# The opening of a mixed conv and attention network: first norm's sums on VectorE, X in two transfers, eight banks, norm vectors first

## The reference

```python
def rms_norm(x, g):
    y = x * lax.rsqrt(jnp.mean(x * x, axis=-1, keepdims=True) + NORM_EPS)
    return y * g

hn = rms_norm(x, a_norm[0])
proj = hn @ a_w_in[0]                     # 1024 x 6144
val, glu_gate, z = jnp.split(proj, 3, axis=-1)
u = val * jax.nn.sigmoid(glu_gate)        # then 31 taps along the tokens, per channel
```

## Time and profile before

| | |
|---|---|
| median of 3 runs | 2649.19 us (2649.11 to 2651.65) |
| the profiled execution, its own time | 2649.69 us |
| its span | 2648.0 us, 31953 instructions |
| busy, share of the span | PE 97%, PEld 79%, DVE 57%, ACT 47%, POOL 57% |
| DMA | 276.51 MB, mean 104 GB/s |

### The profile page before, as it was taken

The page is one execution under the profiler, slowest core; times in us unless marked ns, Lnnn a source line. Parts: engine busy times, 40 slices in busy tenths (PEclk is TensorE's granted clock), DMA queues, the critical chain, the costliest instruction groups (busy, mean ns, idle before and its releaser), DMA issues.

```text
span 2648.0 us, 31953 instructions
## 1 busy us (share of the span) xinstructions
PE 2578.6 (97%) x12164; PEld 2081.0 (79%) x12164; DVE 1521.2 (57%) x2431; ACT 1231.5 (47%) x1939; POOL 1513.8 (57%) x926
## 2 busy tenths in 40 slices
PE   8999999999999899999999999989999999999998
PEld 6877787877777687888888787878877778788887
DVE  4999883145675824444450799976498743523202
ACT  4888544245555534222232598654335553423222
POOL 2799765444444365444455299966635547645652
PEclk9999999999999999999999999999999999999999
DMA  5776424444344123333333577533422242233221
GB/s 145 179 179 145 112 96 87 92 95 70 78 78 69 62 80 87 104 96 96 97 96 103 119 180 170 143 96 96 120 96 71 78 136 100 80 99 101 103 96 48
DMA packets 295128, 276.51 MB, mean 104 GB/s; under 512 B 17653, under 2 KB 258511, under 8 KB 294976
## 3 DMA queue, kind: packets, MB, share of 16 engines
q1 hardware_dynamic: 280880, 223.94, 30.9%
q0 software_dynamic: 14096, 50.53, 9.2%
HBM read 228.75 MB, written 5.84 MB: 89 GB/s over the span
## 4 chain that ended last, share of the span: by engine, by line
PE 84%; DVE 9%; ACT 3%; issue 2%; POOL 1%; DMA 0%; DVEq 0%; POOLq 0%; ACTq 0%
PE ps L64 82%; DVE AR L81 4%; PE ps L67 2%; DVE AR L73 2%; DVE HL L81 1%; ACT L70 1%; ACT HT L70 1%; ACT AR L70 1%; DVE X L73 1%; POOL WL L73 0%; POOL AR L73 0%; DMA AR<-in_x 0%; POOL HL L73 0%; DVE AR L77 0%; ACT HH L70 0%
## 5 line engine op out<-in xcount | busy, mean ns | idle before, releaser
L73 POOL TENSOR_TENSOR WL<-WR,WH 128x1024 fp32r<-128x1024 f32 x329 | 831.9, 2549 | 815.0 <-ACT WH L70 815.0
L64 PE MATMUL ps<-HH,WH 128*128 128x512 f32 x3080 | 1228.8, 399 | 22.9 <-POOL HL L73 12.4
L64 PE MATMUL ps<-HL,WH 128*128 128x512 f32 x3080 | 1202.5, 390 | 0.0
L64 PE MATMUL ps<-HH,WL 128*128 128x512 f32 x3080 | 1100.1, 390 | 0.0
L64 PEld LDWEIGHTS ps<-HH,WH 128*128 128x128 f32 x3080 | 580.2, 188 | 167.3 <-issue 33.0
L64 PEld LDWEIGHTS ps<-HL,WH 128*128 128x128 f32 x3080 | 580.7, 189 | 123.6 <-issue 7.7
L64 PEld LDWEIGHTS ps<-HH,WL 128*128 128x128 f32 x3080 | 580.0, 188 | 122.3
L70 ACT ACTIVATE WH<-WR 128x1024 fp32r<-128x1024 f32 (+1 forms) x405 | 409.0, 1047 | 493.0 <-PE ps L64 439.2
L81 DVE SCALAR_TENSOR_TENSOR ps<-AR,CW,ps 128x512 f32<-128x512 f32 x654 | 454.5, 752 | 8.8 <-ACT ps L70 1.5
L73 POOL TENSOR_TENSOR AR<-AR 128x512 f32<-128x512 f32 x200 | 307.9, 1846 | 11.1 <-ACT AR L70 3.8
L70 ACT ACTIVATE AR<-ps 128x512 f32<-128x512 f32 (+3 forms) x265 | 132.2, 523 | 268.2 <-PE ps L64 169.0
(11 more groups left out here) (169 smaller groups left out, 2255.7 us busy)
## 6 DMA issues: line engine op xcount, KB each, us to landing
WR<-in_a_w_in SPq DMA_DIRECT2D x96, 512.0 KB, 5.2
WL<-WR POOLq DMA_DIRECT2D x76, 512.0 KB, 5.8
WR<-in_c_w_in SPq DMA_DIRECT2D x64, 512.0 KB, 5.3
WR<-in_a_w_out SPq DMA_DIRECT2D x16, 1024.0 KB, 4.8
WR<-in_b_w_in SPq DMA_DIRECT2D x16, 1024.0 KB, 8.5
WR<-in_b_w_in SPq DMA_DIRECT2D x32, 512.0 KB, 12.3
WR<-in_w_mlp_in SPq DMA_DIRECT2D x16, 1024.0 KB, 5.4
WR<-in_w_mlp_out SPq DMA_DIRECT2D x16, 1024.0 KB, 4.9
```

Source lines behind the costliest of these rows:

```text
L64: return Op(None if self.e is None else self.e.matmul(o, l, r, start=first, stop=last, skip_group_check=True))
L73: return Op(None if self.e is None else self.e.tensor_tensor(o, a, b, op))
```

## The change

X comes in two DMAs of 1 MB. The small vectors come right behind X (VA) and behind chunk 0 (VB), with semaphores of their own; chunk 1 comes after them, then the conv rows as before. TensorE turns X by blocks of tokens into all eight banks (`X_BANK`), with no sums between. VectorE squares and sums each block of tokens along its row in one instruction, straight from `XIN`. ScalarE copies tiles 0 to 5 out of the banks and VectorE tiles 6 and 7, after the norm vector. ScalarE loads its root table first and takes the root after three copies. Chunk 0 joins the summed chunks, so its WL comes from a DMA add; ScalarE splits its half 0 after the root and its half 1 inside the loop over HH, after HH 3; the conv taps are copied after HH 1. The turn of the conv taps now stands behind the spread.

```diff
         def summed(i, n):
-            return any(f < i < f + KE + (KE // 2 if n == 0 else 0) for f in FIRST_A)
+            return i == 0 or any(f < i < f + KE + (KE // 2 if n == 0 else 0) for f in FIRST_A)
...
+        X_BANK = [7, 4, 5, 6, 3, 2, 1, 0]
+        BY_SCALAR = 6
         def wait_x(eng, m, k):
             if m == 0:
-                eng.wait_ge(x0, k)
+                eng.wait_ge(*((sq_made, "x", k) if k < BY_SCALAR else (x0, k)))
...
         def mean_square_vector(dve, m):
-            dve.wait_ge(sq_summed, m, KD - 1)
-            rsqrt_vector(dve, ("ms", m), banks[0][:, 0:NB], NB, 1.0 / D)
+            if m:
+                dve.wait_ge(sq_summed, m, KD - 1)
+            else:
+                dve.wait_ge(x0, "sum", NB - 1)
+            rsqrt_vector(dve, ("ms", m), banks[0][:, 0:NB] if m else small(NB, "x_sum"), NB, 1.0 / D)
...
                 act.act(hs(HH, k), tiles[k % 4], ACT.Copy).then_inc(hh, gen, k)
+                if j == 0 and k == 1:
+                    vectors_scalar(act)
+                if j == 0 and k == 3:
+                    split_hi(act, 0, (1,))
...
         def setup_sync(sp):
-            sp.dma(t3(XIN, NB), x[0].rearrange("(b p) d -> p b d", p=P)).then_inc(x_in, by=16)
-            load_chunk(sp, 0)
-            load_chunk(sp, 1)
+            for n in range(2):
+                sp.dma(t3(XIN, NB)[:, 2 * n:2 * n + 2, :],
+                       x[0, 2 * n * P:2 * (n + 1) * P, :].rearrange("(b p) d -> p b d", p=P)).then_inc(x_landed[n], "x", by=16)
             o = 0
             for name, ap, n in VA_ROWS:
-                sp.dma(S_A[o:o + n, :], ap).then_inc(small_in, name, by=16)
+                sp.dma(S_A[o:o + n, :], ap).then_inc(v_landed, name, by=16)
                 o += n
+            load_chunk(sp, 0)
             for n, (name, ap) in enumerate(VB_ROWS):
                 sp.dma(S_B[32 * n:32 * n + 32, :], ap.rearrange("a (k p) -> (a k) p", p=P)).then_inc(
-                    small_in, name, by=16)
+                    v_landed, name, by=16)
+            load_chunk(sp, 1)
...
         def setup_tensor(pe):
             pe.wait_ge(consts, "ident")
-            pe.wait_ge(x_in)
-            for k in range(KD):
-                b = banks[1 + k % 3]
-                if k >= 3:
-                    pe.wait_ge(x0, k - 3)
-                for tb in range(NB):
-                    op = pe.turn(b[:, tb * P:(tb + 1) * P], XIN[:, tb * D + k * P:tb * D + (k + 1) * P], ident[:, :])
-                op.then_inc(xt_made, k)
-                if k:
-                    sum_square(pe, 0, k - 1)
-            sum_square(pe, 0, KD - 1)
-            pe.wait_ge(small_in, "all")
+            for tb in range(NB):
+                pe.wait_ge(x_landed[tb // 2], "x")
+                for k in range(KD):
+                    op = pe.turn(banks[X_BANK[k]][:, tb * P:(tb + 1) * P], XIN[:, tb * D + k * P:tb * D + (k + 1) * P],
+                                 ident[:, :])
+                    if tb == NB - 1:
+                        op.then_inc(xt_made, k)
+            pe.wait_ge(v_landed, VB_ROWS[-1][0])
+            wait_x(pe, 0, X_BANK.index(4))
             pe.turn(banks[4][:, 0:NVA], S_A[0:NVA, :], ident[0:NVA, 0:NVA])
             pe.turn(banks[4][:, 128:224], S_B[0:96, :], ident[0:96, 0:96]).then_inc(vec_turned, "v")
+            wait_x(pe, 0, X_BANK.index(7))
+
+        def vectors_tensor(pe):
+            pe.wait_ge(small_in, "all")
+            wait_x(pe, 0, X_BANK.index(6))
             for j in range(2):
...
         def setup_vector(dve):
             dve.memset(TABLE[32:33, :], NEG).then_inc(tab_neg)
-            for k in range(KD):
+            sums = small(NB, "x_sum")
+            for tb in range(NB):
+                dve.wait_ge(x_landed[tb // 2], "x")
+                row = XIN[:, tb * D:(tb + 1) * D]
+                dve.ttr(SQUARED[tb], row, row, 1.0, 0.0, ALU.mult, ALU.add, sums[:, tb:tb + 1]).then_inc(x0, "sum", tb)
+
+        def rest_of_x_vector(dve):
+            for k in range(BY_SCALAR, KD):
                 dve.wait_ge(xt_made, k)
-                dve.copy(xs(k), banks[1 + k % 3][:, :]).then_inc(x0, k)
+                dve.copy(xs(k), banks[X_BANK[k]][:, :]).then_inc(x0, k)
...
         def setup_scalar(act):
-            for k in range(KD):
-                square(act, 0, k)
-                if k == 3:
-                    split_hi(act, 0)
+            act.wait_ge(consts, "ones")
+            act.act(small(1, "table"), ones[:, 0:1], ACT.Sqrt)
+            for k in range(BY_SCALAR):
+                act.wait_ge(xt_made, k)
+                act.act(xs(k), banks[X_BANK[k]][:, :], ACT.Copy).then_inc(sq_made, "x", k)
+                if k == 2:
+                    rsqrt_scalar(act, ("ms", 0), NB)
+                    split_hi(act, 0, (0,))
...
             normalise_tensor(pe, j)
             if j == 0:
+                vectors_tensor(pe)
                 biases_tensor(pe)
...
             if j == 0:
                 vectors_vector(dve)
+                rest_of_x_vector(dve)
...
-            rsqrt_scalar(act, ("ms", j), NB)
-            if j == 0:
-                vectors_scalar(act)
+            if j:
+                rsqrt_scalar(act, ("ms", j), NB)
             normalise_scalar(act, j)
```

More of the change, by code:

```diff
@@ L691, in build_program @@
         GD = ar(10000, NDIST)
+        SQUARED = [ar(12000 + tb * D, D) for tb in range(NB)]
         SM0 = HT[:, 0:P]
         scratch = nc.dram_tensor("bias_by_distance", (16, NDIST), F32).ap()
+        x_landed = [x_in, sig("s_gin")]
+        v_landed = sig("stored")
         def setup_sync(sp):
-            sp.dma(t3(XIN, NB), x[0].rearrange("(b p) d -> p b d", p=P)).then_inc(x_in, by=16)
-            load_chunk(sp, 0)
-            load_chunk(sp, 1)
+            for n in range(2):
+                sp.dma(t3(XIN, NB)[:, 2 * n:2 * n + 2, :],
+                       x[0, 2 * n * P:2 * (n + 1) * P, :].rearrange("(b p) d -> p b d", p=P)).then_inc(x_landed[n], "x", by=16)
             o = 0
             for name, ap, n in VA_ROWS:
-                sp.dma(S_A[o:o + n, :], ap).then_inc(small_in, name, by=16)
+                sp.dma(S_A[o:o + n, :], ap).then_inc(v_landed, name, by=16)
                 o += n
+            load_chunk(sp, 0)
             for n, (name, ap) in enumerate(VB_ROWS):
                 sp.dma(S_B[32 * n:32 * n + 32, :], ap.rearrange("a (k p) -> (a k) p", p=P)).then_inc(
-                    small_in, name, by=16)
+                    v_landed, name, by=16)
+            load_chunk(sp, 1)
             for j in range(2):
```

## The result

In 20 runs of each on one chip the changed kernel takes 2646.26 us in the median (2645.23 to 2649.90), the kernel before 2651.24 (2649.11 to 2654.64). The ratio is 0.9982, 95% interval 0.9975 to 0.9989: 4.8 us faster, from 2.9 to 6.6. The forecast was 3.8 us faster, 2645.4.

What follows compares the result with a forecast made beforehand. TensorE bounds the kernel, so only the start of its unbroken work counts: its last-tile products end at 40.6 instead of 44.44, 3.8 us less. From the median 2649.19 that gives 2645.4, own range 2643.1 to 2647.4 (chance 0.45).

Steps and rivals of the forecast that it cites:

- The opening's arithmetic: Opening: X's turns from 6.15 to 13.9, sums by 11.7 at worst, root at 14.1, spread ending at 18.2.
- The landing, t = 25.9: Last small rows, awaited by TensorE's turn of the conv taps, land at 25.9 instead of 23.1, 2.8 us for the add.
- the toll: Chunk 0's DMA add overlaps the conv rows' transfers and delays them, between nothing and 2.8 us; taken as 2.8.
- the drip: Conv row transfers (`a_conv_w`) on SP's queue at some 78 GB/s, table and one-hot rows within, taken as 6.65 us.
- The chain after the landing: From 25.9: turns and two copies to 28.55, HH 2 and 3 to 29.85, GpSimd's low parts, HL 7 at 39.2.
- The rival with no toll: The add takes no turns from the conv rows' transfers; time 2645.4 - 2.8 = 2642.6, chance 0.18.
- the one in which the rows don't bind: Conv rows in by 20, only GpSimd's wait for half 1 counts; gain 11.6, 2637.6, chance 0.12.
- The hold: GpSimd's add of chunk 0's half 1 stands ahead of its low parts, HL 7 at 39.2 not 36.6; costs 2.6.
- TensorE's pace: Of TensorE's 21 products from 34.4, 7 at 0.425 us and 14 at 0.229, so the end is at 40.6.
- What is late next: Chunk 2's issue moves from 23.84 to 37.7, landed by 48.5 at worst; 4 us of cover are left.
- The rival of a gain given back: Chunk 2's lateness eats VectorE's and ScalarE's slack; TensorE waits 3.8 us or so in the conv stage; 2649.2, chance 0.17.
- the slower one: SP's ten issues behind the chunks held 2.26 us each, landing at 35.5; 5.8 slower, 2655.0, chance 0.08.

Runs made afterwards that it cites:

- the kernel without the sum: Changed kernel with chunk 0 subtracted by GpSimd again, no DMA add; ratio to before 0.9978 (0.9969 to 0.9987).
- the four that only move the landing: Changed kernel with conv rows ahead of chunk 1 (ratio to before 0.9984), in 112 + 12 (0.9974), rows and tables ahead (0.9965), or four row transfers (0.9958).
- with 112 + 12 rows: Changed kernel with each conv row transfer of 124 rows cut into 112 and 12, 16 transfers; ratio to before 0.9974 (0.9963 to 0.9985).
- with TensorE kept busy: Changed kernel with 16 more matmuls on TensorE, results thrown away, in its idle time before the conv taps' turn; ratio to before 0.9980 (0.9971 to 0.9990).

## Why the prediction was right

**What bounds, and that the gain stays.** Right. TensorE sets the conv stage, and the 3.3 us at 41.26 are 3.3 at 308 and at 2275.

**The opening's arithmetic.** Right in order, and off by 1 us in time, off the path: X landed as forecast (turns from 5.98), but TensorE needed 6.59 us for 32 turns and not 7.75, so the root came at 13.0 and the spread at 15.0, not at 16.1.

**The landing, t = 25.9.** Measured 25.8, from parts that were not all right, so its closeness is in part luck. Without the add the rows landed at 23.5 and not at 23.1, 0.4 later; the toll is 2.3 (shown by the kernel without the sum), not 2.8, 0.5 less. The two errors went against each other. The length of the drip was taken over from the kernel before without a cause; its 124 rows set it. The toll was priced as turns that the drip loses while the add runs. The drip lost none from 17 to 19 us and stood still from 20 to 21, so the size was about right and the way to it was not: turns taken a packet at a time, the rule that the prediction cites, do not show in this trace. The issues of SP are held longer than I thought, the last at 20.45. The chain after the landing took 13.07 us to the end of HL 7 in the changed kernel (13.3 forecast) and 13.07 or 13.08 in the four that only move the landing. Its first step was mis-added: eight turns at 0.223 and a copy of 0.58 make 2.4 us, where the prediction has 2.65, and measured are 2.5. The rival with no toll falls, and so does the one in which the rows don't bind: they were forecast as 2642.6 and 2637.6.

**The hold.** Forecast 2.6, measured 2.8 to 3.1 (first product, HL 7).

**TensorE's pace.** The term that was mis-sized: I took 7 of 21 products at 1.2 GHz, and it was 12. That is 5 x 0.2 = 1.0 us. The 21 began at 33.81 and not at 34.4, which gave back 0.6; 0.3 came on top, since the first of them took 0.60 and not 0.425 and the pace did not rise at once. So the first product ended at 41.26 instead of 40.6.

**What is late next.** Chunk 2 went out at 36.19, and no new wait of TensorE came of it in the conv stage. The rival of a gain given back fell with the positions above, the slower one with SP's issues: ten took 9.6 us (11.18 to 20.81), not 22.6.

The forecast was 3.8 us, the trace shows 3.3 in the opening and 4.2 in the span, the runs 4.8 with 2.9 to 6.6. The 0.9 between opening and span lies behind 2611, with the clock; where the rest of the 4.8 comes from is not shown, since each kernel has one trace. That 2645.4 lies so near the measured 2646.26 is in part luck as well: the prediction started from 2649.19, the median of three runs, 2.1 us below the 2651.24 of twenty, and its gain was 1.0 to 1.2 too small.

## What to carry to other kernels

When an opening is reordered, follow each queue to its last member. A wait on a group of transfers ends with the last one issued, and an in-order engine that takes such a wait in the middle of a loop holds all that is behind it. Moving work between engines gains nothing while the chain runs through a transfer; look at which links the new chain has before tuning those that it no longer has. And cut a transfer so that its number of rows divides well (112 + 12 for 124 here), and into few instructions: shape and count cost 5.8 us of the landing here, more than the whole change brought.

## What the runs showed of the hardware

- Transfers of 124 rows of 512 bytes ran at 78 GB/s; the same bytes as 112 + 12 rows at 207.
- SP's issues take longer when much is queued: one small issue took 2.29 us behind chunk 0, eight row transfers 7.67 us behind chunk 1, and 4.15 in the kernel before, where the chunks' bytes were through at 15.1.
- An add of 512 KB delayed the conv rows of the other queue by 2.3 us. The rows kept their pace of 0.08 MB in a microsecond while the add ran widest, and stood nearly still for a microsecond behind that.
- VectorE's 128x512 product of two operands took 2.88 us beside GpSimd's subtraction, 0.69 without it. Its copies of 128x512 out of a bank took 0.69 beside the same subtraction, in the kernel before.
- In the kernel before the granted clock reads 1.00 while products stand 0.42 us apart; in the changed one it reads 0.50 at the same spacing. The spacing is the safer reading.
- In slot 0 the pace rose behind 12 products in the changed kernel, counted from 33.81, behind 6 in the kernel before, which had had no such idle time, behind 9 with 112 + 12 rows and behind 14 with TensorE kept busy. The 16 extra products raised the clock in the idle time, but not for long.
